# An encoder block on one core: expert rows gathered one by one, or both expert tables multiplied densely

## The reference

```python
def body(xb):
    q = (xb @ w_q).reshape(PEER_TOKEN_BLOCK, PEER_HEADS, 2, PEER_HALF_DIM)
    sc = jnp.einsum('thpd,hpkd->thpk', q, sub_keys).astype(jnp.float32)
    s1, i1 = lax.top_k(sc[:, :, 0], PEER_TOPK)
    s2, i2 = lax.top_k(sc[:, :, 1], PEER_TOPK)
    cand = (s1[..., :, None] + s2[..., None, :]).reshape(PEER_TOKEN_BLOCK, PEER_HEADS, -1)
    cidx = (i1[..., :, None] * PEER_N_KEYS + i2[..., None, :]).reshape(PEER_TOKEN_BLOCK, PEER_HEADS, -1)
    top_s, pos = lax.top_k(cand, PEER_TOPK)
    eidx = jnp.take_along_axis(cidx, pos, axis=-1)
    g = jax.nn.softmax(top_s, axis=-1).astype(xb.dtype)
    u_sel = jnp.take(u_tab, eidx, axis=0)
    hid = jax.nn.gelu(jnp.einsum('thkd,td->thk', u_sel, xb), approximate=False) * g
    v_sel = jnp.take(v_tab, eidx, axis=0)
    return jnp.einsum('thk,thkd->td', hid, v_sel)
```

## Time and profile before

| what | value |
|---|---|
| device time, median of three | 1849.06 us |
| lowest and highest of the three | 1846.94 and 1861.19 us |
| span of the profiled execution, first to last instruction | 1856.5 us |
| busy in that span: PE, DVE, POOL, ACT | 72%, 65%, 62%, 24% |
| DMA moved | 594.24 MB, 320 GB/s over the span |

### The profile page before, as it was taken

How to read it: one execution, slowest core, us unless ns; L and a number is a source line. 1 busy time by engine, 2 the same in 40 slices (tenths; PEclk the granted TensorE clock), 3 DMA queues, 4 the chain that set the end, 5 groups by cost and what they waited for, 6 DMA issues and landing times.

```text
span 1856.5 us, 16630 instructions
## 1 busy us (share of the span) xinstructions
PE 1343.4 (72%) x3547; PEld 631.9 (34%) x3547; DVE 1198.2 (65%) x2864; ACT 439.1 (24%) x1049; POOL 1145.1 (62%) x1034
## 2 busy tenths in 40 slices
PE   6976898985588857666666666766777677766776
PEld 5655465572245532222222222222222222222222
DVE  2237768888998766665665566565665666656564
ACT  2323123343332122122121122112121221212112
POOL 0005645663456647777777767777777677777774
PEclk9987987986698988999999999999999999999899
DMA  9449968996689969999999999999999999999997
GB/s 305 152 139 353 348 238 277 322 346 232 229 300 325 345 228 339 347 365 348 342 365 335 347 330 349 351 352 356 347 364 327 338 372 354 365 342 368 340 360 263
DMA packets 196531, 594.24 MB, mean 320 GB/s; under 512 B 18544, under 2 KB 59512, under 8 KB 196472
## 3 DMA queue, kind: packets, MB, share of 16 engines
q0 software_dynamic: 147456, 536.94, 79.0%
q1 hardware_dynamic: 49016, 56.67, 9.3%
HBM read 591.44 MB, written 2.10 MB: 320 GB/s over the span
## 4 chain that ended last, share of the span: by engine, by line
DMA 26%; issue 14%; PE 12%; DVE 10%; POOL 7%; ACT 1%; DVEq 0%; POOLq 0%
DMA v_ring<-in_peer_v_dram,eidx 15%; DMA u_ring<-in_peer_u_dram,eidx 11%; PE acc L730 6%; DVE u_ring L1208 4%; POOL u_ring L507 4%; PE mm L580 3%; POOL v_ring L515 3%; PE acc L580 1%; DVE onehot L1175 1%; DVE picked L1186 1%; DVE onehot L1182 0%; DVE top_p L1165 0%; DVE top_v L1155 0%; DVE top_v L1162 0%; DVE top_hl L1169 0%
## 5 line engine op out<-in xcount | busy, mean ns | idle before, releaser
L730 PE MATMUL acc<-v_ring,diag 128*128 128x512 f32 x1536 | 802.2, 650 | 366.4 <-DMA v_ring<-in_peer_v_dram,eidx 353.6
L1208 DVE CUSTOM_DVE_ANT_0 u_ring<-u_ring,hn 128x1024 f32<-128x1024 f32 x512 | 619.4, 1224 | 388.4 <-DMA u_ring<-in_peer_u_dram,eidx 386.8
L507 POOL DMA_INDIRECT u_ring<-in_peer_u_dram,eidx x512 | 565.8, 1105 | 471.1 <-DVE hid L1208 185.4
L515 POOL DMA_INDIRECT v_ring<-in_peer_v_dram,eidx x512 | 577.2, 1127 | 226.3 <-issue 118.2
L730 PEld LDWEIGHTS acc<-v_ring,diag 128*128 128x128 f32 x1536 | 278.5, 200 | 889.5 <-issue 790.1
L903 ACT ACTIVATE gel<-hid 128x4 f32<-128x4 f32 x128 | 26.2, 205 | 880.1 <-DVE hid L1208 879.9
L1228 DVE SCALAR_TENSOR_TENSOR h<-v_ring,coef,h 128x1024 f32<-128x1024 f32 x128 | 164.4, 1285 | 4.4 <-DMA v_ring<-in_peer_v_dram,eidx 1.0
L910 ACT ACTIVATE diag<-ident,coef 128x128 f32<-128x128 f32 x384 | 131.7, 393 | 91.8 <-PE acc L730 62.3
L580 PE MATMUL mm<-actT,w_ring 128*128 128x384 f32 x336 | 126.1, 534 | 15.9 <-DMA w_ring<-in_w_in_dram 6.3
L580 PEld LDWEIGHTS mm<-actT,w_ring 128*128 128x128 f32 x336 | 69.3, 211 | 67.7 <-issue 20.9
L572 PE MATMUL mm<-w_ring,actT 128*128 128x256 f32 x304 | 77.0, 412 | 1.9 <-issue 0.8
(11 more groups left out here) (192 smaller groups left out, 1055.2 us busy)
## 6 DMA issues: line engine op xcount, KB each, us to landing
w_ring<-in_w_in_dram SPq DMA_DIRECT2D x18, 1024.0 KB, 11.1
w_ring<-in_peer_w_q_dram SPq DMA_DIRECT2D x16, 1024.0 KB, 8.8
u_ring<-in_peer_u_dram,eidx POOLq DMA_INDIRECT x512, 6.1
v_ring<-in_peer_v_dram,eidx POOLq DMA_INDIRECT x512, 6.2
v_ring<-in_w_in_dram SPq DMA_DIRECT2D x6, 1024.0 KB, 12.3
w_ring<-in_w_out_dram SPq DMA_DIRECT2D x6, 1024.0 KB, 11.3
h<-in_x_dram SPq DMA_DIRECT2D x4, 512.0 KB, 6.5
v_ring<-in_w_out_dram SPq DMA_DIRECT2D x2, 1024.0 KB, 5.0
```

The lines of the kernel that those rows point to most:

```text
L507: nc.gpsimd.indirect_dma_start(out=u_ring[:, c % U_RING, :], out_offset=None, in_=peer_u[0], in_offset=bass.IndirectOffsetOnAxis(ap=eidx[p ...
L515: nc.gpsimd.indirect_dma_start(out=v_ring[:, c % V_RING, :], out_offset=None, in_=peer_v[0], in_offset=bass.IndirectOffsetOnAxis(ap=eidx[p ...
L730: last = nc.tensor.matmul(acc[half][:, :], diag[:, c % COLS, :], v_ring[:, c % V_RING, half * BANK:(half + 1) * BANK], start=(starts and c ...
L1208: nc.vector.tensor_tensor_reduce(out=u_ring[:, c % U_RING, :], in0=u_ring[:, c % U_RING, :], in1=hn[:, :], scale=1.0, scalar=0.0, op0=ALU. ...
```

## The change

The host now hands over the same numbers in other layouts (weights in slabs of 8 KB per partition, u in units with features on the partitions, v in units with experts on the partitions). On the chip:

- The four tiles are one group. All projections, attention, norms, queries and key scores of all tiles run first, then the experts. Column-wise projections and queries stream 512 columns.
- Experts, first table (`expert_scores`): for each pair of tiles (0 and 1, then 2 and 3) the whole u table streams through five 1 MB buffers, 512 experts at a time, and PE computes the score of every expert for every token. ACT copies each 128 x 512 block out of PSUM (`keep_scores`) and SP stores it in a DRAM scratch `s_scr` of 8 MB per tile.
- POOL fetches each chosen score as a single 4-byte cell, 128 cells per indirect DMA, 128 DMAs per tile, eight in flight.
- Gate times gelu of the chosen scores is turned (`turn_picks`). For every token DVE makes two 128 x 128 one-hot matrices (`picks`), PE multiplies them (`weights`, four tokens of 128 columns per group, 32 groups per tile), which gives the token's 128 x 128 table of coefficients over all 16384 experts, and ACT copies it to `wts` (`keep_weights`).
- Second table (`mix_values`): for each pair of tiles the whole v table streams through, and PE multiplies it by the dense coefficients.
- The residual goes to DRAM (`h_scr`) and comes back for the last step; `finish` takes the place of `fin_tile`.

```diff
-GROUPS = [[0], [1, 2, 3]]
-HOSTS = 1
-COLS = 4
-U_RING = 4
-V_RING = 4
-W_RING = 2
+W_RING = 4
+PAIRS = 2
+UNIT = 2048
+UNITS = 5
+E_BLOCK = 512
+STAGED = 4
+TOKENS = 4
+EXP_LAG = 6
+IN_FLIGHT = 8
+W0_AT = 24
...
+            def load_unit(k):
+                if k < UNITS:
+                    sp.wait_ge(mm_full, mm_done(("hT", TILES - 1, 1)))
+                elif k - UNITS >= PAIRS * U_UNITS:
+                    sp.wait_ge(v_used, k - UNITS - PAIRS * U_UNITS + 1)
+                elif (k - UNITS) % 2 == 0:
+                    sp.wait_ge(u_half, (k - UNITS) // 2 + 1)
+                else:
+                    sp.wait_ge(u_full, k - UNITS + 1)
+                if k < PAIRS * U_UNITS:
+                    src = u_units[k % U_UNITS]
+                else:
+                    src = v_units[(k - PAIRS * U_UNITS) % V_UNITS]
+                sp.dma_start(slots[k % UNITS], src).then_inc(unit_in[k % UNITS], 16)
+
+            def store_scores(n):
+                for j in range(2):
+                    k = 2 * n + j
+                    sp.wait_ge(s_copied, k + 1)
+                    sp.dma_start(s_scr[2 * (n // E_BLOCKS) + j][:, n % E_BLOCKS * E_BLOCK:(n % E_BLOCKS + 1) * E_BLOCK],
+                                 s_stage[:, k % STAGED, :]).then_inc(s_out[k % STAGED], 16)
...
-            def gather_u(n, par, c):
...
-                nc.gpsimd.indirect_dma_start(
-                    out=u_ring[:, c % U_RING, :], out_offset=None, in_=peer_u[0],
...
+            for t in range(TILES):
+                pool.wait_ge(xs_ready, xs_no[("norm2", t)])
+                nc.gpsimd.dma_start(h_scr[t], h[:, t, :]).then_inc(spilled, 16)
+
+            cells = [s_scr[t].rearrange("p (e a) -> (p e) a", a=1) for t in range(TILES)]
...
+                for c in range(SLOTS):
+                    k = SLOTS * t + c
+                    if k >= IN_FLIGHT:
+                        pool.wait_ge(hid_in[k % IN_FLIGHT], 16 * (k // IN_FLIGHT))
+                        pool.nop(nofuse=True)
+                    nc.gpsimd.indirect_dma_start(
+                        out=hid[:, t, c:c + 1], out_offset=None, in_=cells[t],
+                        in_offset=bass.IndirectOffsetOnAxis(ap=eidx[:, t, c:c + 1], axis=0)).then_inc(hid_in[k % IN_FLIGHT], 16)
...
-            def peer_group(n, g0, starts, emptied):
-                for c in range(g0, g0 + COLS):
-                    if c == 0 and emptied is not None:
-                        pe.wait_ge(acc_drained, emptied)
-                    pe.wait_ge(v_in[c % V_RING], 16 * (TOPK // V_RING) * n + 16 * (c // V_RING + 1))
-                    pe.wait_ge(diag_done, TOPK * (n - PH * HOSTS) + c + 1)
-                    for half in range(2):
-                        last = nc.tensor.matmul(acc[half][:, :], diag[:, c % COLS, :], v_ring[:, c % V_RING, half * BANK:(half + 1) * BANK],
-                                                start=(starts and c == 0), stop=False, skip_group_check=True)
+            def unit(k):
+                pe.wait_ge(unit_in[k % UNITS], 16 * (k // UNITS + 1))
+                return slots[k % UNITS]
+
+            def expert_scores(n):
+                p = n // E_BLOCKS
+                for half in range(2):
+                    u = unit(2 * n + half).rearrange("p (c e) -> p c e", c=KC // 2)
+                    for j in range(2):
+                        k = 2 * n + j
+                        t = 2 * p + j
+                        if half == 0 and k >= len(u_banks):
+                            pe.wait_ge(s_copied, k + 1 - len(u_banks))
+                        for c in range(KC // 2):
+                            last = nc.tensor.matmul(u_banks[k % len(u_banks)][:, :],
+                                                    actT[:, KC // 2 * half + c, t * P:(t + 1) * P], u[:, c, :],
+                                                    start=(half == 0 and c == 0), stop=(half == 1 and c == KC // 2 - 1),
+                                                    skip_group_check=True)
+                        if half == 1:
+                            last.then_inc(u_full, 1)
+                        elif j == 1:
+                            last.then_inc(u_half, 1)
+
+            def turn_picks(t):
+                pe.wait_ge(coef_done, t + 1)
+                if t > 0:
+                    pe.wait_ge(turn_copied, t)
+                for i, src in enumerate((idx[:, 0, t, :], idx[:, 1, t, :], hid[:, t, :])):
+                    last = nc.tensor.transpose(turn_bank[:, i * P:(i + 1) * P], src, ident[:, :])
+                last.then_inc(turn_full, 1)
+
+            def weights(t, g):
+                k = GROUPS_W * t + g
+                pe.wait_ge(picks_done, 2 * k + 2)
+                if k >= len(w_banks):
+                    pe.wait_ge(w_copied, k + 1 - len(w_banks))
+                for i in range(TOKENS):
+                    last = nc.tensor.matmul(w_banks[k % len(w_banks)][:, i * P:(i + 1) * P],
+                                            picks_c[:, k % 2, i, :], picks_a[:, k % 2, i, :], start=True, stop=True)
+                last.then_inc(w_full, 1)
+
+            def mix_values(p):
+                pe.wait_ge(w_copied, 2 * GROUPS_W * (p + 1))
+                if p > 0:
+                    pe.wait_ge(fin_step, FIN * (2 * p - 1) + 3)
+                for m in range(V_UNITS):
+                    v = unit(PAIRS * U_UNITS + V_UNITS * p + m)
+                    for a in range(2):
+                        i1 = 2 * m + a
+                        for j in range(2):
+                            for half in range(2):
+                                lo = D * a + BANK * half
+                                last = nc.tensor.matmul(acc[j][half][:, :], wts[j][:, i1, :], v[:, lo:lo + BANK],
+                                                        start=(i1 == 0), stop=(i1 == K1 - 1), skip_group_check=True)
                     last.then_inc(v_used, 1)
...
+            for n in range(PAIRS * E_BLOCKS):
+                expert_scores(n)
+                late = n - E_BLOCKS - W0_AT
+                if late >= 0:
+                    if late == 0:
+                        turn_picks(0)
+                    for g in range(late * GROUPS_W // (E_BLOCKS - W0_AT), (late + 1) * GROUPS_W // (E_BLOCKS - W0_AT)):
+                        weights(0, g)
+            for p in range(PAIRS):
+                for t in range(2 * p, 2 * p + 2):
+                    if t > 0:
+                        turn_picks(t)
+                        for g in range(GROUPS_W):
+                            weights(t, g)
+                mix_values(p)
...
+            def keep_scores(n):
+                for j in range(2):
+                    k = 2 * n + j
+                    act.wait_ge(u_full, k + 1)
+                    if k >= STAGED:
+                        act.wait_ge(s_out[k % STAGED], 16 * (k // STAGED))
+                    nc.scalar.activation(s_stage[:, k % STAGED, :], u_banks[k % len(u_banks)][:, :], ACT.Copy).then_inc(s_copied, 1)
...
+                nc.scalar.activation(wts[t % 2][:, :, g * TOKENS:(g + 1) * TOKENS],
+                                     w_banks[k % len(w_banks)][:, :].rearrange("p (t i) -> p i t", t=TOKENS),
+                                     ACT.Copy).then_inc(w_copied, 1)
...
-            def dot(n, par, c):
...
+            def picks(t, g):
+                k = GROUPS_W * t + g
+                if g == 0:
+                    dve.wait_ge(turn_copied, t + 1)
+                if k >= 2:
+                    dve.wait_ge(w_full, k - 1)
+                lo = g * TOKENS
+                nc.vector.tensor_tensor(out=picks_a[:, k % 2, :, :], in0=iota_f[:, :].unsqueeze(1).broadcast_to([P, TOKENS, K1]),
+                                        in1=turned[:, lo:lo + TOKENS].unsqueeze(2).broadcast_to([P, TOKENS, K1]),
+                                        op=ALU.is_equal).then_inc(picks_done, 1)
+                for i in range(TOKENS):
+                    last = nc.vector.tensor_scalar(picks_c[:, k % 2, i, :], iota_f[:, :], turned[:, P + lo + i:P + lo + i + 1],
+                                                   turned[:, 2 * P + lo + i:2 * P + lo + i + 1], ALU.is_equal, ALU.mult)
+                last.then_inc(picks_done, 1)
...
+            for u in range(PAIRS * PH):
+                topk(u)
+            for t in range(TILES):
+                coefs(t)
+                for g in range(GROUPS_W):
+                    picks(t, g)
+                    if t >= 2 and g == GROUPS_W // 2:
+                        finish(t - 2)
+            for t in range(2, TILES):
+                finish(t)
...
+    u_units = u_tab.reshape(blocks, E_BLOCK, 2, kc // 2, p).transpose(0, 2, 4, 3, 1).reshape(2 * blocks, p, kc // 2 * E_BLOCK)
+    v_units = v_tab.reshape(-1, 2, p, d).transpose(0, 2, 1, 3).reshape(-1, p, 2 * d)
```

More of the change, by code:

```diff
@@ L479, in _ @@
[L479 to L487 removed]
+            sp.dma_start(subkT[:, :, :], keys_t).then_inc(keys_in, 16)
@@ L951, in _ @@
+            for t in range(2, TILES):
+                fin_squares(t)
```

1200 lines of the change are left out of this document (515 added, 685 removed).

## The result

The changed kernel takes 2551.0 us (median of four runs, 2549.7 to 2552.5), the kernel before 1855.1 us (median of four on the same chip). The ratio is 1.3745, with a 95% interval of 1.3678 to 1.3812: slower by 37%. The forecast was 2550 us.

What follows compares the result with a forecast made beforehand. The prediction took DMA, fetching 4 KB rows for the gathers, to bound the stretch from 697 us on. Its terms 550 + 878 + 238 + 878 + 17 gave 2561 us of span, by ratio 0.996 2550 us; 80% range 2480 to 2710.

Steps and rivals of the forecast that it cites:

- Part 1: Expert stage: the row fetches and dot products disappear, and with them the whole stretch after 697 us, minus 1159 us.
- Part 2: PE's price for one matmul of 512 columns, read from the old trace: 0.857 us.
- the 0.52 us of the other figure: Price per 512-column matmul if the skill page's sustained 131 ns held: 0.520 us, with a sum near 1750.
- Parts 3 and 5: First and second table: 1024 matmuls each, plus 878 us each; beside the first, loads, copies, topk and cells hidden.
- Part 4: Coefficient tables of the four tiles: DVE bounds each group of four tokens at 1.65 us, plus 238 us together.
- Part 6: The front, all tiles' norms, projections, queries and attention before the tables: 495 us plus waits, so 550 us.
- Part 7: The end: two tiles finished one after the other, a second 8 or 9 us, plus 17 us.
- Slow cells: Rival on POOL's gathers: a gather of cells takes 3 us, so tiles come late, 3025 us in all; 8%.
- A sagging clock: Rival on PE's long dense runs: granted clock means 0.85, 310 us more, 2860 us in all; 5%.
- Cheap long streams: Rival on both tables and the front: long-run matmuls cost 0.514 us, 815 us less, 1735 us in all; 2%.

Runs made afterwards that it cites:

- E9: The kernel before, with the matmuls that add the fetched v rows reading only the upper 16 bits of both operands as bfloat16: 1852.0 us, ratio 0.9989.
- e1: The changed kernel with the second table's product computed for only the first 512 of 1024 output features, same loads: 2111.6 us.
- e4: The changed kernel with every 1 MB table unit also copied from the table to a DRAM scratch: 2553.5 us.
- e2: The changed kernel with every gather of cells issued a second time into a spare column: 2814.0 us.
- e3: The changed kernel with both tables' matmuls reading only the upper 16 bits of both operands as bfloat16: 1659.0 us, 0.892 of the kernel before.

## Why the prediction was right

By its own parts, with what the trace of the changed kernel has (us of span), each part cut where PE's timeline has the last matmul of one and the first of the next:

| part | forecast | measured |
|---|---|---|
| front, to the first line 634 | 550 | 542.1 |
| first table with tile 0's coefficients | 878 + 51 | 930.1 |
| tile 1's coefficients | 61 | 57.2 |
| first pass over the second table | 439 | 439.5 |
| tiles 2 and 3 | 126 | 127.5 |
| second pass | 439 | 439.8 |
| end | 17 | 12.4 |

- **The total** was met in part by luck. The parts add up to 2561 us of span, 12 more than measured. The forecast then took 10 off by the ratio 0.996, which compared the median of before with the span of another execution. In every execution timed here the time is 1.7 to 2.0 us above its own span, so the right step was upward, and the parts stand for 2563 us, 0.5% too high.
- **Part 1, the gathers' stretch goes.** It went. E9 excludes PE's products as its bound; that it was DMA's, as the chain had said, fits the share of 0.94 to 0.95.
- **Part 2, the price of a matmul.** This step carried the forecast, and it held to the third digit: 0.857 us from the earlier trace rows and from e1. Two runs of 4 and 16 matmuls were enough to price 2048, and the 0.52 us of the other figure did not show.
- **Parts 3 and 5, what lies beside them.** Loads were covered up to twice the traffic (e4). Cells came every 1.25 us against 1.24 forecast. The last of pair 0's 256 was issued at 1304 us, before PE stood ready for the first of its two tiles at 1325; e2 shows the wait that appears when they are twice as dear.
- **Part 4, coefficient tables.** DVE bounds a group: 1.63 us against 1.65 taken between 1.5 and 1.9. The `finish` in the middle costs 6.2 us more than a usual wait, against 6. The chains ahead of a tile were 5 us for tile 1, where 8 were forecast, and 11 for tiles 2 and 3 together, where 8 were. Tile 0's share came to 52 us against 51, from 542.1 to 1472.2 less 878.
- **Part 6, the front,** was 8 us too high, the largest error of the sum, and it hides two larger ones: behind the first 29 us PE was busy for 482 us and not 467, and idle for 31 and not 55. **Part 7, the end,** was 5 us too high: the two tiles' finishes follow in 4.6 us and not in 8 or 9, since DVE starts the second sum as soon as the first product is written.
- **The rivals.** Slow cells: real as a mechanism, but the price was 1.25 and not 3. A sagging clock: 0.99 to 1.00 in the table stretches. Cheap long streams: excluded by the 91 matmuls in a run at 0.86 us and by the 0.857 of e1. The back-to-back section of the Trainium skill, "TensorE: Matmul & The Clock Gate", has a sustained 131 ns beside 216 ns for an isolated one of 512 columns. The measured bfloat16 run is at 0.225 us for each matmul, and a float32 matmul at four times 214 ns. The bfloat16 run is near the isolated figure, and neither kind of operand shows the sustained one.

## What to carry to other kernels

Before sparse fetches are replaced by dense products, multiply out both resources: here 594 MB of traffic became 339, against some 1750 us of float32 products on the two tables, and the sign of the change hung on the price of one matmul, which two short runs of the old trace already gave. The dense form pays where the products are cheap (0.225 us and not 0.857), and then its next limits are the table stream and the single-cell gathers. Where two queues' orders are interleaved, ask of every load what it waits for and which load stands behind it: four slab loads, moved by three places, were worth 38 us in one kernel and 41 us in another.

## What the runs showed of the hardware

**A gather takes longer beside DVE's picks.** POOL's timeline in the changed kernel, before and while DVE builds picks:

```profile
989.28 0.95 POOL L474 DMA_INDIRECT hid<-s_scr,eidx  x1 [0.31 <-DMA hid<-s_scr,eidx]
...
1485.26 1.32 POOL L474 DMA_INDIRECT hid<-s_scr,eidx  x1 [0.30 <-issue]
1486.88 1.32 POOL L474 DMA_INDIRECT hid<-s_scr,eidx  x1 [0.30 <-issue]
```

and DVE's in the second of these stretches:

```profile
1485.06 0.70 DVE L1115 TENSOR_TENSOR topk_mem<-iota_f,shared 128x512 f32<-128x512 f32 x1
1485.66 1.13 DVE L1119 TENSOR_SCALAR topk_mem<-iota_f,shared 128x128 f32<-128x128 f32 x4
1486.69 0.70 DVE L1115 TENSOR_TENSOR topk_mem<-iota_f,shared 128x512 f32<-128x512 f32 x1
```

A gather costs 0.94 to 0.95 us alone and 1.32 beside the picks, and then exactly one gather goes per group of DVE, 1.63 us for both. DVE itself loses nothing: in the picks of tile 3, with no gather in flight, a group also takes 1.63 us.

```profile
2042.04 0.69 DVE L1115 TENSOR_TENSOR topk_mem<-iota_f,shared 128x512 f32<-128x512 f32 x1
2042.64 1.12 DVE L1119 TENSOR_SCALAR topk_mem<-iota_f,shared 128x128 f32<-128x128 f32 x4
2043.67 0.69 DVE L1115 TENSOR_TENSOR topk_mem<-iota_f,shared 128x512 f32<-128x512 f32 x1
```

The specifications of the Trainium skill's "GPSIMD Engine Reference" have POOL's SBUF interfaces shared with VectorE, with contention for DVE instructions of two SBUF inputs. Line 1115 is such an instruction, and the trace agrees in that the gather grows by 0.38 us; which of the group's five instructions holds it, no run shows. In the changed kernel this costs nothing. In e2, where the gathers are late, 30 of them beside the picks of tile 1 and 26 beside those of tile 2 were so long, by their durations 22 us in all, and both delay the cells of tile 3, which came 24 us later than expected. That arithmetic fits; it was not tried apart.

**Stream rates.** Table units, with 8 KB contiguous per partition, moved at 410 GB/s over 192 us together with the stores of scores (e3's first pass, its row above), against 347 GB/s for the fetched rows of 4 KB. The two differ in more than the size of the piece, and no run varied that alone.

**The clock in e9.** In e9 the granted clock over 1150 us was 0.50, the 1.2 GHz level, with PE busy a third of the time, against 0.95 with the float32 products. A record cost 390.1 / 753 = 0.52 us of busy time there, against 252.5 / 998 = 0.25 in e3, so much of the gain in price was lost again. The kernel's time did not change for it, with PE idle for 768 us in that stretch.
